# Taking the filler matmuls out of a two-layer hybrid decoder step

## The reference, cut to what matters

```python
for layer in range(2):
    h = rms_norm(x, g_mix[layer])
    if layer == 0:                       # short gated conv beside dilated attention
        y = even_mixer(h, w_in, conv_a_w, w_out, ...)
    else:                                # GLU, causal conv of 31 taps, layer norm, swish, projection
        u = za * sigmoid(zg)             # za, zg = split(h @ w_pw1 + b_pw1)
        c = silu(layer_norm(causal_dwconv(u, dw_w) + dw_b, ln_g, ln_b))
        y = c @ w_pw2 + b_pw2
    x = x + y
    h = rms_norm(x, g_ffn[layer])        # top 1 of 4 groups, then top 2 of 8 experts in it
    x = x + hier_moe(h, routers, w_gate, w_up, w_down)   # 32 SwiGLU experts of 1024 -> 256 -> 1024
y = rms_norm(x, g_final)
```

## Time and profile before

| | us |
|---|---|
| three runs: lowest, median, highest | 1275.76, 1278.84, 1280.82 |
| the profiled execution: its own time | 1286.39 |
| the profiled execution: its span | 1284.6 |
| PE busy, PEld busy | 1098.6, 688.4 |
| DVE, ACT, POOL busy | 377.8, 225.7, 116.9 |
| the fillers' records, busy | 51.0 in 136 records |

### The profile page before, as it was taken

The page is one execution under the profiler, slowest core; times in us unless marked ns, Lnnn a source line. Parts: engine busy times, 40 slices in busy tenths (PEclk is TensorE's granted clock), DMA queues, the critical chain, the costliest instruction groups (busy, mean ns, idle before and its releaser), DMA issues.

```text
span 1284.6 us, 18797 instructions
## 1 busy us (share of the span) xinstructions
PE 1098.6 (86%) x7117; PEld 688.4 (54%) x7118; DVE 377.8 (29%) x710; ACT 225.7 (18%) x402; POOL 116.9 (9%) x168
## 2 busy tenths in 40 slices
PE   5999998899869977787749999989969978898990
PEld 4887685676445434344328776754435544454440
DVE  2000012342251111111154899733261211111116
ACT  4000110344201101101141101134111111011112
POOL 1000000100010100000031211100001101111003
PEclk9999997899879989989879999999979999899995
DMA  9623024700467999999972110060095999999966
GB/s 379 268 92 144 30 85 70 292 1 9 160 249 273 412 412 411 413 411 412 393 242 79 67 66 1 16 238 21 33 376 199 412 402 396 402 350 394 412 233 233
DMA packets 79855, 304.78 MB, mean 237 GB/s; under 512 B 8416, under 2 KB 8448, under 8 KB 77600
## 3 DMA queue, kind: packets, MB, share of 16 engines
q1 hardware_dynamic: 54576, 242.76, 48.2%
q0 software_dynamic: 8784, 31.48, 6.9%
q10 hardware_dynamic: 16416, 29.45, 6.6%
HBM read 269.85 MB, written 33.83 MB: 236 GB/s over the span
## 4 chain that ended last, share of the span: by engine, by line
PE 51%; DMA 24%; DVE 11%; issue 9%; ACT 4%; POOLq 0%; POOL 0%; DVEq 0%; ACTq 0%; SPq 0%
DMA ring<-w_moe 15%; PE psum L1442 10%; DMA ar<-w_moe 7%; PE psum L1625 6%; PE psum L1548 6%; PE psum L1757 5%; DVE ar L1307 4%; PE psum L1436 3%; PE psum L1719 3%; PE psum L1680 2%; PE psum L1493 2%; PE psum L1653 2%; DVE X L1060 1%; PE psum L1509 1%; PE psum L1380 1%
## 5 line engine op out<-in xcount | busy, mean ns | idle before, releaser
L1625 PE MATMUL psum<-ring,ar 128*64 128x256 f32 x1408 | 180.0, 401 | 31.3 <-DMA ring<-w_moe 29.6
L1625 PEld LDWEIGHTS psum<-ring,ar 128*64 128x64 f32 x1408 | 102.0, 143 | 106.2 <-DMA ring<-w_moe 35.7
L1442 PE MATMUL psum<-ar,ring 128*128 128x272 f32 x576 | 132.7, 393 | 0.0
L1757 PE MATMUL psum<-ar,ring 128*128 128x272 f32 x512 | 120.8, 397 | 3.0 <-DVE ar L1293 3.0
L1442 PEld LDWEIGHTS psum<-ar,ring 128*128 128x128 f32 x576 | 109.3, 190 | 22.9 <-issue 0.3
L1757 PEld LDWEIGHTS psum<-ar,ring 128*128 128x128 f32 x512 | 97.8, 192 | 28.0 <-issue 4.2
L1307 DVE SCALAR_TENSOR_TENSOR ar<-ar,sv 128x512 f32<-128x512 f32 x120 | 107.0, 893 | 5.8 <-ACT ar L860 1.9
L1236 DVE COPY ar<-psum 128x128 f32<-128x128 f32 x64 | 18.7, 292 | 281.2 <-PE psum L1670 281.2
L1625 PE MATMUL psum<-ar 128*64 128x256 f32 x640 | 84.9, 409 | 18.6 <-DMA ar<-w_moe 18.6
L1680 PE MATMUL psum<-ring,ar 128*64 128x512 f32 x352 | 84.1, 598 | 0.8 <-DVE ar L1236 0.4
L1548 PE MATMUL psum<-ring,ar 128*128 128x512 f32 x192 | 84.1, 594 | 0.0
(11 more groups left out here) (209 smaller groups left out, 1154.4 us busy)
## 6 DMA issues: line engine op xcount, KB each, us to landing
ring<-w_moe SPq DMA_DIRECT2D x44, 3072.0 KB
ar<-w_moe SPq DMA_DIRECT2D x20, 3072.0 KB, 17.6
expert_outputs<-ar ACTq DMA_DIRECT2D x128, 128.0 KB
ring<-w_mix SPq DMA_DIRECT2D x4, 3072.0 KB, 13.6
ring<-w_pw SPq DMA_DIRECT2D x6, 2048.0 KB, 10.8
ring<-kv_in SPq DMA_DIRECT2D x2, 2880.0 KB, 11.6
expert_outputs<-ring POOLq DMA_DIRECT2D x8, 512.0 KB, 11.4
normed_rows<-ar ACTq DMA_DIRECT2D x8, 512.0 KB, 2.6
```

The costliest lines, as they stand in the source:

```text
L1442: t = mm(psum[:, b + h, 0:HALF], w[:, k, P * c:P * c + P], hT[:, k, HALF * h:HALF * h + HALF], start=k == 0, stop=k == KD - 1)
L1625: t = mm(psum[64 * f:64 * f + 64, u % 2, 0:2 * P], xt[:, k, 64 * (u % 2):64 * (u % 2) + 64], w[:, k, f, :], start=k == 0, stop=k == KD - 1)
L1757: t = mm(psum[:, b + h, 0:HALF], w[:, k, o:o + P], hT2[:, k, HALF * h:HALF * h + HALF], start=k == 0, stop=k == KD - 1)
```

## The change

The function `stay_warm` and its five calls are taken out. They made 68 fillers in all: one after each of the five tiles of norm 0, twelve and seven in each of the two routings, three after each of the five tiles of norm 2, and ten in the layer norm. Nothing else is changed, and what is left on every engine stands in the same order.

```diff
-            def stay_warm(times, bank=0):
-                for _ in range(times):
-                    mm(psum[:, bank, 0:C_SM], ident, cst[:, 0:C_SM], start=True, stop=True)
-
             for i in range(TILES):
                 turn(0, i)
-                stay_warm(1, 6)
             pe.wait_ge(hT_ready, 10)
...
                 mm(psum[:, 6, 0:160], cst[:, C_TRI:C_TRI + P], mk, start=True, stop=True).then_inc(moe.ranks, 1)
-                stay_warm(12)
                 pe.wait_ge(moe.places, n + 1)
...
                 t.then_inc(moe.table, 1)
-                stay_warm(7)
                 pe.wait_ge(moe.jobs, n + 1)
...
             for i in range(TILES):
                 turn(2, i)
-                stay_warm(3, 6)
             pe.wait_ge(hT_ready, 30)
...
             t.then_inc(var_done, 1)
-            stay_warm(10, 6)
             for c in range(2):
                 pe.wait_ge(later_w[c], 32)
```

## The result

The kernel without the 68 fillers is slower: a median of 1291.38 us (8 runs, 1287.0 to 1296.42) against 1281.82 (8 runs, 1275.76 to 1286.8) of the kernel before, a ratio of 1.008 with a 95% interval of 1.0053 to 1.0108. That is +10.2 us (the interval allows 6.8 to 13.8), where 6.9 were forecast. The profiled execution of the kernel after took 1292.31 us with a span of 1290.5; that of before took 1286.39 with 1284.6. So the sizes are taken from means over the executions of several kernels, and the single pair serves to see the mechanism.

The account below looks back on a forecast made before the run. TensorE's own work on the chain and expert transfers were taken to set the pace, filler busy time being no saving; terms 1.6 + 1.9 + 0 + 0.5 + 2.9 = +6.9 on 1278.84 gave 1285.7 us, range 1278 to 1293.

Parts of the forecast that it names:

- later behind the landing of the gathered rows: Sign in the routings: the first expert reload is issued some 1.6 us later after the gathered rows land.
- some 8: Sign in the experts: the first 52 records take some 8 us in both layers.
- I take +0.3, near the lower end: Routing table's 40 small matmuls: low clock adds +0.3 us, from a possible 0 to +1.46.
- The upper bounds of the routings: Largest losses allowed for the two routings: +3.9 us in layer 0, +5.0 in layer 1.
- The 1.32 already lost goes: Layer 0's first expert matmuls: 1.32 us already lost at low clock with fillers, credited as -1.3.
- 7.0 forecast: Routings: low clock lasts 7.0 us from the start of the gathered rows' transposes, into the expert matmuls.
- Until 675.07 + 4.3 = 679.4: Norm 2: the projection runs at the low clock until 679.4 and loses 1.35 us.
- The hold: Norm 2: fillers kept the projection waiting; without them it begins 1.3 us earlier, at 676.7.
- With 4.3 us of low clock it loses 1.35: Norm 0: 4.3 us of low clock from the last turn's start costs the input projection 1.35 us.
- The clock is back before it matters: Rival, all five places: holds of 2.5 us go, low stretches end within the transposes; 1276.4 us, chance 0.12.
- The experts absorb their part: Rival: the two routings give nothing, only norm 0, norm 2 and layer norm count; +2.1, 1280.9 us, chance 0.20.
- The low clock stays: Rival: projections and experts begin with 9 us of low clock; +15, 1293.8 us, chance 0.13.

Follow-up runs that it names:

- no_route: The kernel before with only the 38 fillers of the two routings taken out; 1285.62 us, ratio 1.0036.
- no_norm2: The kernel before with only the 15 fillers of norm 2 taken out; 1281.81 us, ratio 1.0007.
- no_norm0_ln: The kernel before with only the 5 fillers of norm 0 and the 10 of the layer norm taken out; 1286.38 us, ratio 1.0028.
- keep12: The kernel before with only the seven fillers behind the table taken out, in both routings; 1285.99 us, ratio 1.0034.
- keep7: The kernel before with only the twelve fillers behind the ranks taken out, in both routings; 1283.88 us, ratio 1.0026.
- no_hold: The kernel before without fillers behind the last turns of norm 0 and norm 2, and two, not three, behind norm 2's fourth; 1280.26 us, ratio 0.9995.
- norm0_last: The kernel before with one filler out, the one behind the fifth turn of norm 0; 1281.54 us, ratio 0.9994.
- attn_fill: The kernel before with six fillers added around the samples' attention and before the second block of scores; 1275.07 us, ratio 0.9949.
- more_fill: no_hold with fillers added in the attention, norms with a router, ranks, routings and last convolution block of layer 1; 1263.22 us, ratio 0.9851 against the kernel before.
- more_fill2: more_fill with the filler behind the fifth turn of norm 0 put back; 1265.41 us, ratio 0.9867 against the kernel before.
- small_fill: The kernel before with all 68 fillers kept, each on a 32x32 corner of the array; 1329.53 us, ratio 1.035.

## Why the forecast's direction held and its size was low

The measured side of each term is the mean of the stage over the executions with and without its fillers (out of: before, after, no_route, no_norm2, no_norm0_ln, keep12, keep7, no_hold, norm0_last, attn_fill, as far as their edit leaves the stage alone):

| term | forecast | measured | how |
|---|---|---|---|
| norm 0 | +1.6 | +2.2 | last turn to the end of the projection, 91.15 (after) and 92.33 (no_norm0_ln) against 89.5 |
| routing, layer 0 | +1.9 | +3.0 | 24.36 (after, no_route) against 21.3 |
| norm 2 | 0 | +1.05 | 54.69 (after, no_norm2) against 53.6; last turn to the end of the projection, 41.34 and 40.08 against 39.5: +1.2 |
| layer norm | +0.5 | +0.7 | some 7.35 against 6.66, swish to projection |
| routing, layer 1 | +2.9 | +3.3 | 24.4 against 21.1 |
| sum | +6.9 | +10.2 | ratio 1.008 of 1281.82: +10.2 (6.8 to 13.8) |

The median of 1291.38 is 5.7 above the forecast of 1285.7: 3.0 because the kernel before measured 1281.82 in this comparison and not the 1278.84 of its three runs, and 2.7 because the two medians are 9.6 apart and not 6.9. It lies just above the forecast's own range (1281 to 1291) and inside the whole one (to 1293). That the sum of the terms meets the 10.2 so well is partly luck, for each rests on two executions without the fillers.

*The mechanism was right.* The transposes behind the gathers took 1.97, the projections began with a low stretch, and the experts did not give the delay back (no_route +4.6 us). The reload did come "later behind the landing of the gathered rows": from the transposes to the reload it took 15.19 us in after against 14.42 in before in layer 0, and 15.11 against 13.24 in layer 1. The first 52 expert records took 7.3 us in after, and the "some 8" came in no_route.

*"I take +0.3, near the lower end", for the table.* Wrong: it is +1.02, in both layers and in no_route. The 22 ns that are not columns in a small matmul are also slower at the low clock: 40 took 2.48 us, 62 ns each, 1.70 times 36. Twice 0.7 is 1.4 of the missing 3.3 us, and the largest mis-sized term.

*The upper bounds of the routings* don't come out of their terms: 1.46 + 0.81 + 2.5 - 1.3 is 3.5 and not 3.9, and in layer 1 it is 4.5 and not 5.0. The measured terms lie inside either.

*"The 1.32 already lost goes", in layer 0.* This was the chance of one execution. Routing 0 took 22.38 in before's, and 20.50 to 22.06 in five others with the same fillers. As a credit for the median it was wrong, and with the table it makes the whole miss of layer 0. The low stretch itself was sized well: 7.0 forecast; from the start of the transposes it was 7.1 to 7.3 us in no_route (0.50 up to 386.9, 1.00 from 387.1), 5.9 and 5.7 in after. Its ground was weaker than it looked. One of the two stretches behind the 7.0, the 7.9 us from 343.45, was misread: the transposes at 343.45 ran at 1.00 (1.09 us, which the prediction uses as its measure of the full clock), the clock fell behind them, and this stretch was no longer than 6.8 us. That after was below it explains why its terms for the expert records are +1.4 and not +2.1.

*"Until 675.07 + 4.3 = 679.4", in norm 2.* The hold went as worked out: from the start of the last turn to the projection 2.64 us became 1.44, in no_norm2 too. But the clock stayed low to 682.8, 7.4 us behind the last turn's start at 675.39, and so the 160 records lost 3.23 and not 1.35. In no_norm2 it was low for some 4.9 us from that turn's start, and they lost 1.97. So the 4.3 was too short here in both, by 0.6 and by 3.1. Whether the turn with its gap, like the transposes with a gap ahead of the experts, makes the stretch longer is not shown: between 4.9 and 7.4 chance can do as much.

*"With 4.3 us of low clock it loses 1.35", in norm 0.* In after the low stretch ended some 4.4 us behind the turn's start, as assumed, and from the last turn to the end of the projection the term is 91.15 - 89.5 = +1.6, just the forecast. The turn went to 1.06 in place of an estimated 1.23 (0.68 + 0.55), so the projection began 0.2 sooner than worked out and lost 1.71. In no_norm0_ln the stretch lasted some 7 us and the term was +2.8. The right size in after was in part luck.

*The rivals.* "The clock is back before it matters" fell at all five places. "The experts absorb their part" fell with no_route and with the stages behind the first reloads. "The low clock stays", with 9 us or more, did not happen in the projections or experts (the longest, 8.4 us, stood in keep12 behind the transposes at 380.30), and the measured +10.2 lies between the forecast's +6.9 and its +15.

By the Trainium skill, "TensorE: Matmul & The Clock Gate", Part 1, one and the same kernel has a different count of slow matmuls from run to run; the table of stages agrees, with 88.27 to 89.96 and 101.91 to 108.89 us for the same code. The same section puts the price of the ramp below 1% of the span of a typical kernel. The 0.8% of the 68 fillers lies below it, though its interval reaches 1.08%. For all low stretches of this kernel together it seems too low, since more_fill gained 1.49% (1.17 to 1.81) over a kernel that already had fillers, of which some 0.1% is the hold of norm 2.

*Why the pair shows 5.9 of 10.2.* Before's execution lost 1.7 us more than after's in the attention (108.89 to 107.20), 1.4 in layer 0's router (the first stage up to the places 56.04 to 54.63), and 1.3 in routing 0; these are as large as the terms looked for. Against it after's stage from the first projection to the second, ahead of the layer norm, was 2.6 us longer (161.56 to 158.97), of which the layer norm is 0.65. Of the other 1.9, some 0.9 lies in the last convolution block's sum and the sums of squares behind it, where after's clock was 0.50 from 853.6 to 860.3 and before's only from 853.2 to 856.4; 1.0 lies in the taps ahead of them and is not explained. Other executions with other edits were low there for as long or not at all, so it isn't put down to the change.

*Where more_fill's 1.49% (19.1 us) comes from.* Against the means of the others: attention 8.3, layer 0's router 2.8 (52.82 against 55.6), layer 1's 2.7 (88.03 against 90.7), norm 2 1.8, routing 0 0.7, and input projection -2.0, in sum 14.3. Some 4.8 us aren't assigned; its last stage, from the first reload of layer 1 to the end, took 295.45 against 297.3 to 301.0 elsewhere, and as more_fill2 took 301.03 there, that looks like chance.

## What to carry to other kernels

Count idle time of TensorE not as free but by what runs behind it: where it waits some microseconds for another engine, and its own work on the chain follows, this work starts at half clock, and here it cost 0.7 to 3.3 us a place and 0.8% in five. A filler belongs right ahead of that work, must use the whole array (32x32 did not do), and should end before the operands of the work are there; one that outlasts the wait gives back as hold what it saves in clock. Look through the granted clock of the whole kernel before tuning fillers one by one, and judge a term of 1 to 2 us by several executions, for one stage varies by as much; and cut the stage narrowly, from the last event ahead of the change to the first behind it.

## What was not expected of the hardware

- The largest loss of all was not behind idle time but in work: in the attention TensorE was busy for 22.66 of 27.00 us, with 112 of 155 records on 32 columns of the array (48 of them on 32 rows too), and had 0.50 throughout. In small_fill it was busy for 34.12 of 35.00 with fillers of 32x32, and had 0.50 too. Busy time by the profile is no sign that the clock will hold. Whether in the attention it was the narrow records or the gaps between the others isn't shown: in keep7 the same 112 narrow records ran at 1.00, and the clock fell behind them.
- How long the attention is at 0.50 is chance, in part: its stage took 101.91 to 108.89 us in ten executions of kernels with the same code there, and 98.98, 98.99 and 98.97 in the three with six fillers.
- A small matmul (16 or 32 columns) went from 36 to 62 ns at the half clock, 1.70 times; eight transposes from 1.09 to 1.97, 1.81 times; the attention's records above from 2.07 to 3.80, 1.84 times.
- What stays open: how much of a low stretch's length (2.8 to 8.4 us behind the starts looked at) is chance and how much the pattern of the work at its start.
